# A sparse-attention stage whose query tiles are walked from the middle of the sequence outwards

## The reference

```python
logits = jnp.einsum('bqhgd,bqkhd->bqhgk', qg, k_sel) * (HEAD_DIM ** -0.5)
logits = jnp.where(valid[:, :, None, None, :], logits + bias, -jnp.inf)
p = jax.nn.softmax(logits, axis=-1)
o = jnp.einsum('bqhgk,bqkhd->bqhgd', p, v_sel)
```

## Time and profile before

| | us |
|---|---|
| median of three runs | 3347.75 |
| lowest and highest | 3340.59, 3351.28 |
| the profiled execution: its own time | 3348.67 |
| the profiled execution: its span | 3346.9 |
| attention stage, from its first instruction to the next stage's | 1826.8 to 2716.2 |
| first chunk on VectorE, first turned pair on VectorE | 1843.55, 1865.11 |
| TensorE, VectorE, ScalarE, GpSimd busy over the span | 96%, 79%, 44%, 38% |

### The profile page before, as it was taken

The page is one execution under the profiler, slowest core; times in us unless marked ns, Lnnn a source line. Parts: engine busy times, 40 slices in busy tenths (PEclk is TensorE's granted clock), DMA queues, the critical chain, the costliest instruction groups (busy, mean ns, idle before and its releaser), DMA issues. The chain is left out here.

```text
span 3346.9 us, 50085 instructions
## 1 busy us (share of the span) xinstructions
PE 3205.9 (96%) x19053; PEld 2955.4 (88%) x19053; DVE 2660.2 (79%) x3935; ACT 1466.9 (44%) x1961; POOL 1282.5 (38%) x1144
## 2 busy tenths in 40 slices
PE   7999999999999999999998999999999989999998
PEld 4999888999999999999998777777777879899987
DVE  2442788998989899999997899999999965885444
ACT  2321566997950110001001677777777730432121
POOL 3322111454334410000000686786966744674200
PEclk8999998999999999999999999999999999999999
DMA  6465534445555653344444533434433355477343
GB/s 222 144 187 168 148 117 133 150 159 171 177 188 174 232 204 134 133 171 174 168 152 146 126 84 91 109 78 106 98 86 86 82 187 189 158 236 259 128 148 112
DMA packets 401941, 502.96 MB, mean 150 GB/s; under 512 B 61008, under 2 KB 316688, under 8 KB 400101
## 3 DMA queue, kind: packets, MB, share of 16 engines
q1 hardware_dynamic: 346021, 304.59, 31.7%
q10 hardware_dynamic: 44352, 149.49, 12.6%
q0 software_dynamic: 11392, 46.68, 3.5%
HBM read 310.63 MB, written 184.27 MB: 148 GB/s over the span
## 5 line engine op out<-in xcount | busy, mean ns | idle before, releaser
L1140 PE MATMUL psum<-ha,gt 128*128 128x352 f32 x8136 | 1353.3, 325 | 6.5 <-DVE ha L1414 4.4
L1140 PEld LDWEIGHTS psum<-ha,gt 128*128 128x128 f32 x8136 | 1323.0, 189 | 10.7 <-DVE ha L1414 4.7
L1450 DVE SCALAR_TENSOR_TENSOR cv<-cv,vecs,cv 128x1056 f32<-128x1056 f32 (+1 forms) x480 | 607.7, 1345 | 0.0
L1999 ACT CAST at<-psum 128x1024 fp32r<-128x1024 f32 (+2 forms) x308 | 289.5, 940 | 211.1 <-PE psum L1932 209.2
L1932 PE MATMUL psum<-ident,at 128*128 128x128 f32 (+1 forms) x2320 | 345.1, 272 | 14.9 <-DVE at L2064 12.6
L1932 PEld LDWEIGHTS psum<-ident,at 128*128 128x128 f32 (+1 forms) x2320 | 273.7, 140 | 94.6 <-issue 21.9
L1111 POOL TENSOR_TENSOR gt<-gt,ones 128x1024 fp32r<-128x1024 f32 x60 | 123.1, 2052 | 609.6 <-PE psum L1140 609.6
L717 PE MATMUL psum<-br,br 128*128 128x352 f32 x2016 | 339.5, 329 | 13.8 <-DVE br L2437 9.2
L2064 DVE TENSOR_TENSOR at<-psum,at 128x1024 fp32r<-128x1024 f32 (+2 forms) x308 | 346.0, 1126 | 7.9 <-ACT at L1999 7.4
L717 PEld LDWEIGHTS psum<-br,br 128*128 128x128 f32 x2016 | 332.3, 191 | 18.1 <-issue 10.2
L1271 ACT ACTIVATE gt<-psum 128x1056 f32<-128x1056 f32 x80 | 84.0, 1049 | 599.7 <-PE psum L1140 599.7
(11 more groups left out here) (251 smaller groups left out, 4231.8 us busy)
## 6 DMA issues: line engine op xcount, KB each, us to landing
scratch_ws<-gt SPq DMA_DIRECT2D x112, 512.0 KB, 4.0
gt<-scratch_ws ACTq DMA_DIRECT2D x110, 512.0 KB, 4.8
gt<-in_w_in_dram SPq DMA_DIRECT2D x60, 512.0 KB, 5.8
scratch_gm<-gt ACTq DMA_DIRECT2D x32, 528.0 KB, 3.0
br<-scratch_gm ACTq DMA_DIRECT2D x32, 528.0 KB, 3.7
scratch_m<-br POOLq DMA_DIRECT2D x32, 528.0 KB, 4.9
at<-scratch_q SPq DMA_DIRECT2D x128, 128.0 KB, 3.1
scratch_u<-gl POOLq DMA_DIRECT2D x16, 528.0 KB, 4.3
```

What stands on the lines that cost most here:

```text
L1140: return nc.tensor.matmul(of[:, j, 0:W // 3], part[:, c, :], a[:, c, j * (W // 3):(j + 1) * (W // 3)], start=(c == 0 and k == 0), stop=(c ...
L1450: ins = nc.vector.scalar_tensor_tensor(to[:, 0:width], mine[:, k_:k_ + width], tap, to[:, 0:width], ALU.mult, ALU.add)
L1999: nc.scalar.copy(phi[j % 3][:, 0:len(mine), 0:n], turned[j % 2][:, 0:len(mine), 0:n]).then_inc(s_phi, 1)
```

## The change

The tiles of a group are walked in the turned order 7, 8, 6, 9, 5, 10, ... 0, 15, and then the sample. The units' places in the room of score rows are put to match: a tile below 8 now lies at the end of its half, the others and the sample at its start, and the side changes after every tile below 8 and after tile 15. All tables that the steps are made of follow from the order by the same rules as before. The group's number of chunks (172), of pairs (77) and all instructions of a unit stay as they are.

```diff
-    TILES = [t for k in range(NT // 2) for t in (k, NT - 1 - k)] + [NT]
+    TILES = [t for k in reversed(range(NT // 2)) for t in (k, NT - 1 - k)] + [NT]
...
             n = self.blocks[u]
-            if t == NT:
+            if t < NT // 2:
+                self.place.append(half * side + half - n)
+            else:
                 self.place.append(half * side)
-                side = 1 - side
-            elif t < NT // 2:
-                self.place.append(half * side)
-            else:
-                self.place.append(half * side + half - n)
+            if t < NT // 2 or t == NT - 1:
                 side = 1 - side
```

## The result

The changed kernel takes 3363.19 us, the median of six runs (3352.71 to 3366.32), where the kernel before took 3345.14 in six runs beside it. The ratio is 1.0045, 95% interval 1.0034 to 1.0057: slower by about 15 us, where a gain was forecast, and above the range. In it the attention stage lasts from 1814.9 to 2728.4, 913.5 us where it was 889.5; the stages ahead of it happened to be 11.8 us shorter than in the profile of before. By the profiles the stage is 24.0 us longer, by the timed runs some 15.

The account below looks back on a forecast made before the run. The prediction took VectorE to set the attention stage's pace, with TensorE right behind it. Its terms, -4.3 - 3.3 - 2.4 + 1.6 + 1.0 = -7.4 us, took 3348.67 to 3341.3, given as 3341, range 3331 to 3351.

Parts of the forecast that it names:

- VectorE's fixed work plus its idle time: Attention stage: VectorE sets the pace and keeps every instruction, so only its idle stretches change the time.
- The start: Start of the attention stage: beginning with tile 7 shortens VectorE's early waits; -4.3 us, bounds -5 and -2.5.
- The border: Borders between groups: waits of 6.6 us go, 2.4 behind tile 14 and 0.9 at the sample come; -3.3 us.
- Two units that close together: Step 92 and once in group 3: VectorE's waits for GpSimd behind the slow moved half go; -2.4 us.
- Chained chunks: Chunks taking the minimum of the chunk right ahead start 0.12 us later; 13 more such chunks, +1.6 us.
- The tail: Behind the last chunk: TensorE sets the step for four full pairs before the sample's; +1.0 us, bounds 0.5 and 2.5.
- The sum: All terms for the attention stage together: -7.4 us, from 3348.67 to 3341.3.
- GpSimd falls behind: Rival: key splits beside tiles 3, 2 and 1 overload GpSimd, three groups lose 19 us; 3360, chance 0.10.
- its turning point: VectorE's finish of tile 10 (step 32): GpSimd's fold due there is done some 1.4 us ahead, so barely hidden.
- the sign that I named for it: VectorE's waits for GpSimd, rows or folds, exceeding 3 us would show the forecast wrong.
- Waits come back elsewhere: Rival: bunched light and heavy steps bring waits that cancel all but the start and the sure losses; 3346, chance 0.22.
- TensorE gets ahead: Rival: more three-chunk steps let TensorE fill its ring, half of the 18.4 us product waits may go; 3331, chance 0.12.

Follow-up runs that it names:

- e3: Changed kernel with the low part of the next group's values issued ahead of head 3's row instead of head 2's at tile 9: stage 911.2 us, ratio 1.0056.
- e1: Changed kernel with VectorE's finish as a reciprocal of all the sums, product with the gates left out: stage 1074.2 us, ratio 1.0559.
- e2: Kernel before with VectorE's finish as a reciprocal of all the sums, product with the gates left out: stage 1078.0 us, ratio 1.0566.
- e8: Kernel before with tiles 7 and 8 put first in the first head group only: stage 894.2 us, ratio 1.0001.
- e11: Changed kernel with the finish as a short reciprocal (gates left out) and GpSimd's key and value splits mostly cut to a few columns: stage 880.9 us, ratio 0.9959.
- e12: Kernel before with the finish as a short reciprocal (gates left out) and GpSimd's key and value splits mostly cut to a few columns: stage 876.2 us, ratio 0.9945.
- e9: Changed kernel with GpSimd's key and value splits for later groups mostly cut to a few columns, finish as it is: stage 905.8 us, ratio 1.0037.
- e10: Kernel before with GpSimd's key and value splits for later groups mostly cut to a few columns, finish as it is: stage 887.1 us, ratio 0.9986.
- e4: Changed kernel with every unit's finish on GpSimd instead of VectorE, nothing left out: stage 894.9 us, ratio 1.0006.
- e7: Kernel before with every unit's finish on GpSimd instead of VectorE, nothing left out: stage 911.6 us, ratio 1.0072.

## Why the prediction was wrong, point by point

**"VectorE's fixed work plus its idle time"** is the step that failed. The work was not fixed: +15.7 us in the finishes, of which gains account for 15.5 and the parts for 6.8, with less behind query splits and rows. The idle time, forecast to fall by 7.4 in all, rose by 5.5. The sum has no term for the finish's price, since the change left it in place. The rows to read were those of one operation with very different durations: the finish of 64x512 took from 0.65 to 1.78 us before, while a remainder of 128x1024 took 1.21 to 1.23 and a chunk of 512 keys 0.66 to 0.75. The rule also treats TensorE and GpSimd as followers. e3 shows that most of the time saved on VectorE comes back as idle time; only in e1 and e2, with VectorE loaded by 142 and 158 us more, does the rule hold.

**The start (-4.3).** Right as a measure, worth nothing as time. VectorE waits 4.7 us for products instead of the 3.5 forecast, and the first remainder comes 33.7 us into the stage instead of 38.35. But by the end of group 0 the waits are 20.5 against 21.1, and e8, which has this term alone, is at 1.0001. The clock did dip in the lead-in, to 0.67 and 0.50 in the two windows from 1834 to 1838 (0.50 is the 1.2 GHz level), right behind a window in which TensorE was busy 0.74 of 2 us. That is ahead of the idle products, which start at 1837.38, and not behind them, where the prediction looked for it:

```profile
1832.00:1834.00 2.00, 0.74 (x2) 0.30 (x2) 1.84 (x6) 0.84 (x1) 0.00 (x0) 1.00 1.12 229
1834.00:1836.00 2.00, 1.99 (x5) 1.25 (x6) 1.88 (x6) 2.00 (x4) 1.51 (x3) 0.67 0.84 156
1836.00:1838.00 2.00, 2.00 (x7) 1.60 (x7) 1.69 (x7) 1.99 (x3) 1.92 (x3) 0.50 0.00 0
```

VectorE lost 0.2 to it there.

**The border (-3.3).** The 6.6 went as said: no wait for ScalarE of 1.2 and none of 1.20 behind step 76, 0.3 each instead. What came was mis-sized. Behind tile 14 I put 2.4 and the trace has 3.3 (0.42 to 1.06 behind step 63 in each of four groups, and 0.94 behind step 62 in one; three more of 0.24 there are not counted). At the sample's pairs I put 0.3 a border and the trace has 1.6, and the 0.3 behind step 76: 5.6 over three borders in place of 0.9. The term is +2.3.

**Two units that close together (-2.4).** Right: VectorE's wait for L1861's counterpart is gone.

**Chained chunks (+1.6).** Called sure, and small: chunks with their reading instructions take 491.6 us instead of 491.4, and gaps of up to 0.15 us sum to 25.2 instead of 24.7, so 0.7 and not 1.6.

**The tail (+1.0).** The last chunk stands 20.9 us ahead of the next stage, about 20 was forecast, and it was 17.7. VectorE's waits from step 71 to 75 of the last group are 3.1 us instead of 2.8, so the loss is nearer 0.3 than 1.0.

**The sum.** With hold and parts taken away (e11, e12), which leaves what my terms spoke of, the turned order is 4.7 us slower, not 7.4 faster. Most of these 12 us are the border (5.6) and waits of 0.3 to 0.8 at steps 29, 46, 54, 55, 64 and 67 of a group, which I had taken to cancel against others. The remaining 19 us of the 24 are the hold and the parts; by the ratios it is 10 of 15 (0.0014 is left of 0.0045).

**The rivals.** *GpSimd falls behind* was given 0.10 and 3360, and it is the one that came nearest, at 3363. That its number came near is in part luck. Its place was right for the first three groups (the parts among the small tiles), but group 3, which has none, lost as much, and its turning point was wrong: I looked at the fold that VectorE waits for, and what gave way was the query split behind the part, and the finish that overlaps it. I called 1.4 us of slack enough, with costs that stand for each operation alone. Nor did the sign that I named for it come: VectorE waits 0.3 us for rows and not over 3, since a held finish counts as busy and a late query split shows as a wait for products. *Waits come back elsewhere* holds for the border and the start. *TensorE gets ahead* didn't happen: waits for products rose by 7.5 us instead of falling by 9.

Still open: why the finishes meet the gains so much more often in the turned order, and why the hold costs more there once the parts are small (24.9 us of stage from e11 to e9, against 10.9 from e12 to e10), while the finishes differ by 17.0 and 10.9. TensorE's longer waits for remainders point to its having less in hand there, but no run separates that. Single profiles are only good to some us, but the ratios say the same (0.0078 and 0.0041).

## What to carry to other kernels

A change of order also moves every operation whose place was fixed by hand against the old order: list them, and look which instruction of another engine each will now meet. An engine that is about 80% busy (GpSimd, 78.8 of 100 us in the earlier trace rows) is not slack if its long operations stand ahead of short ones that others need within a step. Try their places, and the engine of each operation, before the order is judged. Here the verdict on the order turned round with the finish's engine (e4 against e7), and with that the places of the parts were worth 48 us. And before "this work is fixed" carries a sum, look at the spread of each operation's durations, not at its mean.

## What the runs showed of the hardware that was not expected

A VectorE product of two SBUF tiles of 64x512 takes 0.65 to 0.69 us alone and up to 4.99 beside GpSimd. It can lose to a GpSimd operation that starts behind it (0.86 us behind it in group 2, 0.40 in group 3). A reciprocal of one tile was not held once (0.748 mean, none above 0.8, in four kernels). GpSimd pays too: its row addition is 0.67 alone and 1.11 to 1.19 where it starts 0.2 to 0.3 behind a finish. VectorE's reciprocal costs 3.34 us for 64x512 and 0.76 for 64x100. The same product of 64x512 on GpSimd takes 1.29, and VectorE's chunks and remainders keep their durations beside it (438.4 and 347.1 us in all in e4, 437.3 and 346.8 in the changed kernel). Chunks and remainders, which have one operand in PSUM, show no such spread in any order.
